# Four heads per interruption of TensorE in the attention, and a last weight chunk multiplied by row tile and column half ahead of each LayerNorm

## The reference, cut to what matters

```python
for i in range(DEPTH):                       # DEPTH = 2
    y = swa_sink_attention(...) if i % 2 == 0 else forgetting_attention(...)
    x = layer_norm(ALPHA * x + y, ln_g[i, 0], ln_b[i, 0])
    y = conv_ffn(x, w_up[i], conv_w[i], conv_b[i], w_down[i])
    x = layer_norm(ALPHA * x + y, ln_g[i, 1], ln_b[i, 1])
# in both mixers, per head and block of 128 queries:
#   p = exp(s - m);  p /= sum(p) (+ exp(sink - m));  o = p @ v
```

## Time and profile before

| | |
|---|---|
| median of three runs | 2142.12 us (2141.55 to 2143.27) |
| the profiled execution | 2144.39 us, of which the span from first to last instruction is 2142.6 us |
| PE busy | 2127.8 us, 99% of the span |
| DVE, ACT, POOL busy | 63%, 49%, 10% |
| granted clock of PE, mean | 0.999 of full speed |
| DMA, mean | 190 GB/s |

### The profile page before, as it was taken

The page is one execution under the profiler, slowest core; times in us unless marked ns, Lnnn a source line. Parts: engine busy times, 40 slices in busy tenths (PEclk is TensorE's granted clock), DMA queues, the critical chain, the costliest instruction groups (busy, mean ns, idle before and its releaser), DMA issues.

```text
span 2142.6 us, 40679 instructions
## 1 busy us (share of the span) xinstructions
PE 2127.8 (99%) x15160; PEld 1953.6 (91%) x15160; DVE 1341.0 (63%) x1829; ACT 1043.8 (49%) x1396; POOL 219.4 (10%) x211
## 2 busy tenths in 40 slices
PE   9999999999999999999999999999999999999998
PEld 8887899999999988888998997899999999988887
DVE  5676676766666654546576676576766666655554
ACT  4554465555555543335445444365555455544332
POOL 2000002220000000000251330002230000000000
PEclk9999999999999999999999999999999999999999
DMA  8554567666666656565665664657766666666563
GB/s 275 158 187 138 177 188 213 201 203 195 191 193 194 193 191 195 192 193 159 199 197 186 186 201 155 195 157 206 203 209 195 192 190 195 193 212 193 196 192 123
DMA packets 206603, 407.67 MB, mean 190 GB/s; under 512 B 12832, under 2 KB 13408, under 8 KB 206400
## 3 DMA queue, kind: packets, MB, share of 16 engines
q1 hardware_dynamic: 199680, 384.35, 58.6%
q0 software_dynamic: 5984, 20.74, 3.4%
q10 hardware_dynamic: 864, 1.57, 0.3%
HBM read 404.44 MB, written 2.18 MB: 190 GB/s over the span
## 4 chain that ended last, share of the span: by engine, by line
PE 96%; DVE 2%; ACT 1%; DMA 1%; issue 0%; DVEq 0%; ACTq 0%
PE ps L1302 19%; PE ps L1304 18%; PE ps L1305 18%; PE ps L1284 12%; PE ps L1286 12%; PE ps L1285 12%; PE ps L1477 1%; PE ps L1499 1%; PE ps L1486 1%; PE ps L1386 0%; PE ps L1410 0%; DMA raw<-in_a_w_o_dram 0%; DVE cg L882 0%; DVE w_lo L827 0%; PE ps L1508 0%
## 5 line engine op out<-in xcount | busy, mean ns | idle before, releaser
L827 DVE TENSOR_TENSOR w_lo<-raw,w_hi 128x1024 fp32r<-128x1024 f32 x725 | 914.7, 1267 | 618.3 <-ACT w_hi L534 616.6
L534 ACT ACTIVATE w_hi<-raw 128x1024 fp32r<-128x1024 f32 x725 | 768.6, 1060 | 929.5 <-PE ps L1305 489.1
L1302 PE MATMUL ps<-xh,w_lo 128*128 128x256 f32 x3572 | 993.6, 278 | 2.9 <-DVE xl L878 1.8
L1305 PE MATMUL ps<-xh,w_hi 128*128 128x256 f32 x3572 | 987.2, 276 | 0.0
L1304 PE MATMUL ps<-xl,w_hi 128*128 128x256 f32 x3572 | 987.2, 276 | 0.0
L1302 PEld LDWEIGHTS ps<-xh,w_lo 128*128 128x128 f32 x3572 | 670.6, 188 | 13.8 <-issue 8.1
L1305 PEld LDWEIGHTS ps<-xh,w_hi 128*128 128x128 f32 x3572 | 671.2, 188 | 0.0
L1304 PEld LDWEIGHTS ps<-xl,w_hi 128*128 128x128 f32 x3572 | 670.7, 188 | 0.0
L1286 PE MATMUL ps<-w_hi,hid_h 128*128 128x512 f32 x704 | 273.9, 389 | 0.0
L1285 PE MATMUL ps<-w_hi,hid_l 128*128 128x512 f32 x704 | 273.9, 389 | 0.0
L1284 PE MATMUL ps<-w_lo,hid_h 128*128 128x512 f32 x704 | 273.9, 389 | 0.0
(11 more groups left out here) (188 smaller groups left out, 1407.3 us busy)
## 6 DMA issues: line engine op xcount, KB each, us to landing
raw<-in_ffn_w_up_dram SPq DMA_DIRECT2D x352, 512.0 KB, 4.3
raw<-in_ffn_w_down_dram SPq DMA_DIRECT2D x176, 512.0 KB, 4.7
raw<-in_b_w_qkvf_dram SPq DMA_DIRECT2D x96, 512.0 KB, 4.3
raw<-in_a_w_qkv_dram SPq DMA_DIRECT2D x39, 512.0 KB, 4.3
raw<-in_a_w_o_dram SPq DMA_DIRECT2D x32, 512.0 KB, 4.4
raw<-in_b_w_o_dram SPq DMA_DIRECT2D x32, 512.0 KB, 4.7
bias<-rel_by_distance POOLq DMA_DIRECT2D x4, 1024.0 KB, 6.9
bias<-minus_cumulated_decay POOLq DMA_DIRECT2D x4, 1024.0 KB, 6.3
```

The source lines that it names most:

```text
L534: act.activation(w_hi[:, loc % RING], raw[:, loc % RING], ACT.Copy).then_inc(high_ready, 1)
L827: dve.tensor_tensor(w_lo[:, s], raw[:, s], w_hi[:, s].bitcast(FP32), ALU.subtract).then_inc(low_ready, 1)
L1302: pe.matmul(o, w_lo[:, slot, k % 2, cols], xh[:, k, :], start=(k == 0 and j % 2 == 0), stop=False, skip_group_check=True)
L1305: last = pe.matmul(o, w_hi[:, slot, k % 2, cols], xh[:, k, :], start=False, stop=(k == KT - 1), skip_group_check=True)
```

## The change

Three things.

1. **The attention is placed by fours.** PE's calls stand after slots 1, 5, 7, 11 and 13: scores of pairs 0 and 1; transposes of four heads; scores of pairs 2 and 3 and values of pairs 0 and 1; transposes of four heads; `turn_sums` and values of pairs 2 and 3. Scores and transposed probabilities of four heads now need four banks each. The sink's exponentials come after the fourth head's own instead of ahead of each head's, under a new semaphore. On DVE, `out_copy(1)`, `out_norm(1)` and `out_low(0)` move behind slot 14's split, and on ACT `spread_sums(1)` and `out_high(1)` move from slots 11 and 14 to 12 and 15. The output projection no longer waits for the whole third group before its first slot.
2. **The last two chunks ahead of a norm are multiplied by row tile and column half.** The last four k tiles are done for rows 0 to 127, then for rows 128 to 255 and the left 256 columns, then for the right 256 columns into another bank. DVE takes the statistics of the first row tile and of the left half meanwhile; after the last product it adds the right half, takes statistics of 256 columns and aggregates one row tile instead of two.
3. **The down projection's loop of two column groups is written out in PE's stream**, so that only the last group is ordered in this way.

```diff
+SCORES_AT = (1, 7)
+TURNED_AT = (5, 11)
+VALUES_AT = (7, 13)
...
+            def score_bank(j, idle):
+                return (S_BANK, S_BANK + 1, 2 * idle, 2 * idle + 1)[j % 4]
+            def turned_bank(j):
+                return (PT_BANK, S_BANK, S_BANK + 1, O_BANK)[j % 4]
...
+            def sink_exponentials(q, hc):
+                act.wait_ge(sinks_ready, 1)
+                for j in range(4):
+                    s = 4 * q + j
+                    ins = act.activation(esink[:, q, :, j], nmax[:, :, s], ACT.Exp, bias=sinks[:, 0, hc + s:hc + s + 1])
+                ins.then_inc(esinks_ready, 1)
...
             def attention_slot(k, hc, quads, kt, sink):            # ACT
+                for q in range(2):
+                    at = SCORES_AT[q]
+                    if k == at + 1:
+                        exponentials(4 * q, hc)
+                    if k == at + 2:
+                        exponentials(4 * q + 1, hc)
+                        exponentials(4 * q + 2, hc)
+                    if k == at + 3:
+                        exponentials(4 * q + 3, hc)
+                        if sink:
+                            sink_exponentials(q, hc)
...
             def attention_slot(k, hc, quads, kt, group, sink, idle):   # DVE
+                for q in range(2):
+                    at = SCORES_AT[q]
+                    if k == at:
+                        reduce_scores(4 * q, hc, group, sink, idle)
+                        reduce_scores(4 * q + 1, hc, group, sink, idle)
+                    if k == at + 1:
+                        reduce_scores(4 * q + 2, hc, group, sink, idle)
+                    if k == at + 2:
+                        reduce_scores(4 * q + 3, hc, group, sink, idle)
                 if k == 9:
                     one_over_sums(0, hc, sink)
+                    out_copy(0, hc, quads)
                 if k == 11:
                     one_over_sums(1, hc, sink)
+                for q in range(2):
+                    if k in (TURNED_AT[q], TURNED_AT[q] + 1):
+                        for c in range(2):
+                            copy_probs(4 * q + 2 * (k - TURNED_AT[q]) + c, hc)
...
             def residual(s, turn, used, n, pieces, tile0=0):       # DVE, rows 128 to 255
+                        if tile0 and half == 1:
+                            dve.wait_ge(chunks_used, used)
+                            dve.tensor_tensor(res[:, 1, part], res[:, 1, part], ps[:, RIGHT_BANK, 0:SEQ], ALU.add).then_inc(last_whole, 1)
+                            dve.wait_ge(last_whole, tile0)
+                        last = dve.bn_stats(stats[:, 1, bass.ds(n * 2 + half, 1), :].rearrange("p a b -> p (a b)"), res[:, 1, part])
...
             def group(s, turn, b4, loc0, lh, ll, nk=KT, before=None, tile0=None):   # PE
-                    if tile0 is last_tile0 and k >= nk - 2:
+                    if tile0 is last_tile0 and k >= nk - 4:
                         if k == nk - 1:
-                            for m in range(MT):
-                                for kk in (k - 1, k):
-                                    last = product(s, turn, kk, nk, lh, ll, loc % RING, tile0, (m,))
+                            for kk in range(nk - 4, nk):
+                                product(s, turn, kk, nk, lh, ll, (loc0 + kk // 2) % RING, tile0, (0,))
+                            for kk in range(nk - 4, nk):
+                                last = half_product(bank(s, 1)[:, 0:SEQ], 0, kk, False, kk == nk - 1, lh, ll, (loc0 + kk // 2) % RING)
+                            last.then_inc(last_left, 1)
+                            for kk in range(nk - 4, nk):
+                                last = half_product(ps[:, RIGHT_BANK, 0:SEQ], 1, kk, kk == nk - 4, kk == nk - 1, lh, ll, (loc0 + kk // 2) % RING)
+                                if kk % 2 == 1:
+                                    last.then_inc(chunks_used, 1)
...
             def scores(q, hc, quads, kv, first_waits, idle):       # PE, both pairs of a half
+                    pe.wait_ge(scores_used, hc + 4)
+                    pe.wait_ge(probsT_ready, hc + 4)
...
             def attention_slot(k, hc, quads, kv, first_waits, idle):   # PE
+                for q in range(2):
+                    if k == TURNED_AT[q]:
+                        for j in range(4):
+                            turn_probs(4 * q + j, hc, quads)
+                    if k == SCORES_AT[q]:
+                        scores(q, hc, quads, kv, first_waits, idle)
+                if k == VALUES_AT[0]:
+                    for i in (0, 1):
+                        times_values(i, hc, quads, kv)
+                if k == VALUES_AT[1]:
+                    pe.wait_ge(scores_used, hc + HG)
+                    pe.wait_ge(probsT_ready, hc + HG)
+                    turn_sums(0, quads)
+                    turn_sums(1, quads)
+                    for i in (2, 3):
+                        times_values(i, hc, quads, kv)
```

More of the change, by code:

```diff
@@ L595, in turned_copy, with exponentials @@
                    .then_inc(acc_free[s][0], 1)
-            def exponentials(s, hc, sink):
+            def exponentials(s, hc):
                 act.wait_ge(scores_used, hc + s + 1)
                 q, j = s // 4, s % 4
[L601 to L604, removed]
                 act.activation(prob[:, s % 4, 0:P], prob[:, s % 4, 0:P], ACT.Exp, scale=-1.0, bias=nmax[:, 0, s:s + 1],
@@ L1015, in residual @@
                     dve.wait_ge(acc_free[s][m], turn + 1)
-                    last = dve.bn_stats(stats[:, m, bass.ds(n, 1), :].rearrange("p a b -> p (a b)"), res[:, m, cols])
+                    if m == 0:
+                        last = dve.bn_stats(stats[:, 0, bass.ds(n, 1), :].rearrange("p a b -> p (a b)"), res[:, 0, cols])
+                        if tile0:
+                            own.link(last)
+                            last = dve.bn_aggr(mv[:, 0, :], stats[:, 0, 0:OUT_GROUPS, :].rearrange("p a b -> p (a b)"))
+                    for half in range(2 if m == 1 else 0):
+                        part = bass.ds(n * COLS + half * SEQ, SEQ)
+                        if tile0 and half == 1:
[3 more added lines that the diff above has]
+                        last = dve.bn_stats(stats[:, 1, bass.ds(n * 2 + half, 1), :].rearrange("p a b -> p (a b)"), res[:, 1, part])
+                        if half == 0:
+                            own.link(last)
                 return last
@@ L1035, in layer_norm @@
                 own.link(last)
[L1036 to L1038 removed]
+                own.link(dve.bn_aggr(mv[:, 1, :], stats[:, 1, :, :].rearrange("p a b -> p (a b)")))
                 dve.tensor_scalar(var[:, :], mv[:, :, 1], LN_EPS, None, ALU.add).then_inc(var_ready, 1)
@@ L1225, in mlp @@
                 for n in range(1, OUT_GROUPS):
-                    residual((n - 1) % 2, (t0, t1)[(n - 1) % 2] + (n - 1) // 2, CH_DOWN[l] + n * FC, n - 1, pieces)
+                    last = residual((n - 1) % 2, (t0, t1)[(n - 1) % 2] + (n - 1) // 2, CH_DOWN[l] + n * FC, n - 1, pieces)
+                    if l == DEPTH - 1:
+                        own.link(last)
                     if l < DEPTH - 1:
@@ L1276, in _, with product @@
         def _(pe):
-            def product(s, turn, k, nk, lh, ll, slot, tile0=None, tiles=range(MT)):
+            def product(s, turn, k, nk, lh, ll, slot, tile0=None, tiles=range(MT), right_ends=None):
                 for m in tiles:
@@ L1285, in product @@
                     pe.matmul(o, ll[:, k, rows], w_hi[:, slot, k % 2, :], start=False, stop=False)
-                    last = pe.matmul(o, lh[:, k, rows], w_hi[:, slot, k % 2, :], start=False, stop=(k == nk - 1))
+                    last = pe.matmul(o, lh[:, k, rows], w_hi[:, slot, k % 2, :], start=False, stop=(k == nk - 1 or m == 1 and k == right_ends))
                     if k == nk - 1 and m == 0 and tile0:
@@ L1289, in product, with half_product @@
                 return last
+            def half_product(o, half, k, start, stop, lh, ll, slot):
+                cols = slice(half * SEQ, (half + 1) * SEQ)
+                rows = slice(P, 2 * P)
+                pe.matmul(o, lh[:, k, rows], w_lo[:, slot, k % 2, cols], start=start, stop=False, skip_group_check=True)
+                pe.matmul(o, ll[:, k, rows], w_hi[:, slot, k % 2, cols], start=False, stop=False, skip_group_check=True)
+                return pe.matmul(o, lh[:, k, rows], w_hi[:, slot, k % 2, cols], start=False, stop=stop, skip_group_check=True)
             layer = [0]
@@ L1465, in turn_tok, with scores @@
                 last.then_inc(tok_turned, 1)
-            def scores(i, hc, quads, kv, first_waits):
-                if i == 0:
+            def scores(q, hc, quads, kv, first_waits, idle):
+                if q == 0:
                     first_waits()
```

105 lines of the change are left out of this document (42 added, 63 removed).

## The result

The changed kernel takes **2128.42 us** (median of four runs, 2127.3 to 2130.98). The kernel before, run beside it, takes 2142.69 (four runs, 2141.55 to 2143.54). The ratio is 0.9935, with a 95% interval of 0.9918 to 0.9953: 0.65% faster. The forecast was 2128.5. The profiled execution took 2127.92 us, of which the span is 2126.1.

A forecast was written before the change was run, and what follows sets the result against it. PE's stream bounds the kernel (busy 99%). Attention 10.6, layer 0's wait 1.1, `ol` 0.5 and norms 1.4 sum to 13.6 us, off a median of 2142.1: 2128.5 us, range 2126.5 to 2131 (2134.5 with the start-up and table-load rivals).

The forecast's parts named there:

- attention, runs instead of pairs, and layer 0's wait: Attention on PE: 1.32 us less per turn over eight turns, 10.6; layer 0's wait within transposes gone, 1.1.
- wait for `ol`: Ahead of the output projection's first slot: PE's single 0.5 us wait goes, as only groups finished earlier are asked for.
- norms: Ahead of the norms: 0.33 us gained on each of the first three, 0.45 at the last, together 1.4.
- a turn after: Attention on PE after the change: 10.0 us per turn, 9.03 and `turn_sums`, alike in both layers.
- The rival that pays start-up for each pair: Score and value pairs in the attention: each pays full start-up, 5.6 us less gain, 2134.1; chance 0.10.
- The slack: Attention: 0.9 us to spare before the fourth head's transposes, 1.3 between the last copy and slot 7's scores.
- Both rivals that needed a wait here: PE waits for four copies at 16 points: half a microsecond each, about 2136.5 (0.05); 0.85 each, 2142 (0.03).
- the rival of the split: DVE's split behind slot 4 or 10, held by ACT, delays the copies: 1.2 lost at each of 16, 2147.7; chance 0.05.
- Two of the three steps: Norms: half-width products take 2.71 us; variance at 1.6 after the dummies' start; table load holds the root until 1.95.
- 24 of 256 columns at 0.113 stand for twelve of 512: Ahead of the norms: splitting the products adds nothing on PE; the 24 take 2.71 us.
- The rival in which ACT stays closed for as long again: First three norms: a second 1.28 behind the table load puts the root at 3.2, 3.8 us in all, 2132.3; chance 0.03.

The follow-up runs named there:

- experiment 8: The changed kernel with the old wait for the whole third group put back ahead of the output projection's first slot; 2128.37 us (one execution).
- experiment 4: The changed kernel with its transposes two slots earlier, after slots 3 and 9; 2139.73 us (ten runs), ratio 0.9985 to before.
- experiment 2: The kernel before with parts 2 and 3 of the change and the attention's calls as they were; 2143.16 us (ten runs), ratio 1.0001.
- experiments 7, 9 and 10: The changed kernel with, in turn, half-width products reordered (2128.69 us), their rows from the first row tile (2128.65), both runs reading the left columns (2129.97).
- experiments 6 and 11: The changed kernel with ACT's table load ahead of its last split before the first three norms; 2129.63 us (one execution), then 2127.71 (five runs).

## Why the prediction was right

| term | forecast | measured |
|---|---|---|
| attention, runs instead of pairs, and layer 0's wait | 10.6 + 1.1 | 11.74 |
| wait for `ol` | 0.5 | 0.70 |
| norms | 1.4 | 1.0 |
| behind the last norm | nothing | 0.6 |
| sum | 13.6 | 14.0 |
| a turn after | 10.0 | 10.13 |

**The attention.** The step on which most of it hung was a row that the trace of before didn't have, a pair of scores directly behind a pair. It was taken at 0.65, its streaming. Measured: eight score matmuls cost 0.85 and sixteen 1.51, so the second pair 0.66; values 0.80 and 1.45, so 0.65. The rival that pays start-up for each pair is refuted. Twelve transposes with the product behind them in 1.23, the step from the last to the product 0.03, as forecast. A turn of layer 1 is 1.28 shorter (forecast 1.32), one of layer 0 by 0.32 more (forecast 0.27). Layer 0's turns now cost what layer 1's do: the wait inside the transposes has gone with its distance of four slots.

**The wait for `ol`.** It is gone, as forecast, but only 0.28 of its 0.70 through the relaxed condition, which the prediction gave as the reason (experiment 8); the other 0.4 came with `out_low` being earlier.

**Nothing waits for the four.** The slack was forecast at 0.9 for the fourth head's transposes and 1.3 for the copies. Measured: 99.1 less 97.26 is 1.8, and 102.25 less 100.59 is 1.7. Both rivals that needed a wait here are refuted; experiment 4 shows the price when the slack is used up (10.0 us). Of the rival of the split nothing came in the changed kernel; with the transposes a slot earlier a split was late twice, by 0.9 at most, beside POOL's work and not behind ACT's.

**The norms.** Two of the three steps held: the variance at 1.60 (forecast 1.6), the root held by the table load until 1.92 (1.95), a gain of 0.36 and at the last norm 0.49 (0.33 and 0.45). The mis-sized term is "24 of 256 columns at 0.113 stand for twelve of 512": they are 0.120 apart, which takes 0.6 us back. The net is 1.0 instead of 1.4. What the end of the program gained behind the last norm (0.6) had no term in the sum.

**The table load.** The rival in which ACT stays closed for as long again had 1.28 more behind each load. The rows show a load of 1.28 from 250.20 and the root at 251.50, 0.02 behind it. The drain that the Trainium skill ("ScalarE: Activation LUTs", What ACT_TABLE_LOAD costs) adds to a load would have put the root near 252.9 (an estimate with that section's 1.38); no load in these traces shows it: wherever an instruction was due behind one, it started 0.01 to 0.02 later.

**What was luck.** 14.0 lies this near to 13.6 because 0.4 too much at the norms nearly cancels 0.2 too little at `ol` and the 0.6 at the end that was not forecast. That the median fell within 0.1 of the forecast is luck too: it was 2128.42, and the same kernel in another five runs had 2129.1. The start of the program alone moves a run by up to 2 us.

## What to carry to other kernels

Switching TensorE between long streams and short foreign work cost here 0.23 us for each interruption and a start-up of 0.15 to 0.20 for each run of scores or values, and a second pair in the run paid neither: collect the short work as far as the other engines' results and the banks allow, and read from the timeline how much slack is left before the first of them is late. When a feeding engine is late, look at what ran beside it before you blame its queue: a split that takes 1.2 us alone took up to 2.9 beside POOL. An edit that splits a matmul in two should be charged by the measured rhythm of the new shape in its place, since a stream elsewhere with the same shape may run faster (0.113 against 0.120 here).

## What was not expected of the hardware

**DVE's splits slow down beside POOL.** In the kernel after, the split of 128 x 1024 takes 1.22 on average where POOL is idle during it (623 of 725), and 1.74 where POOL is busy for nine tenths of it or more (41), up to 2.92. The prediction charged 1.2 throughout; the distance of two chunks to PE nearly always covers the rest. The Trainium skill ("SBUF — State Buffer", Who interferes with whom) says that a DVE instruction with two SBUF inputs contends with a GpSimd instruction that reads SBUF; the split has two such inputs, and the traces agree with it as far as these durations go. No experiment here took POOL's work away.

**The rhythm of equal products differs by place.** Products of 256 columns come 0.113 apart in most stretches, 0.118 in some (in the turn shown, 47 distances from 92.58 to 98.11: 5.53 us), and 0.120 in the half-width ones, but for the first one or two distances of each norm (0.113 and 0.119). A stretch keeps its rhythm until the next interruption or wait, and the same stretch can have another one in another execution: the 192 products from 1101 on come 0.113 apart in the kernel before, and in experiment 2 at 0.113 up to a short wait and at 0.118 behind it. Over the whole program the slower distances cost 4.7 us in the kernel before, 4.5 in the kernel after and 7.3 in experiment 2 (turned and plain products together). For the half-width ones, most weight loads are reported as 192 ns long instead of 188. Their order, the rows and the columns are excluded by experiments 7, 9 and 10; the cause of either slower rhythm stays open.

**The first 5 to 11 us run slower, for a length that differs from one execution to the next.** PE's timeline of the kernel before, and then of the kernel after, near the start:

```profile
7.69 1.05 PE L1410 MATMUL ps<-w_hi,xl 128*128 128x512 f32 x2
8.54 1.05 PE L1410 MATMUL ps<-w_lo,xh 128*128 128x512 f32 x2
```

```profile
7.21 0.63 PE L1465 MATMUL ps<-w_hi,xl 128*128 128x512 f32 x2
7.67 0.63 PE L1465 MATMUL ps<-w_lo,xh 128*128 128x512 f32 x2
```

Two products of 512 columns take 0.85 in the first and 0.46 in the second. The view prints a granted clock of 1.00 for both stretches, but for the first that is no reading: the trace's record of the full clock begins at 10.34 us in the kernel before and at 5.14 in the kernel after, and there is none ahead of it. In the 14 traces it begins between 4.9 and 11.2 us. In the seven where it begins at 8.7 or later, neighbouring products are 0.43 apart ahead of it and 0.23 behind it; in the seven others it begins at 6.74 or sooner, and none are 0.43 apart. These distances stand to one another nearly as TensorE's two levels do, 1.2 and 2.4 GHz, so I read the slow stretch as the lower level, though no row says so. PE did the same in both kernels up to 4.5 us: dummies from 1.54 on.

It is not the change's: the kernel of experiments 6 and 11, the same program, came to the same product after 40.61 us in one execution and after 38.89 in the other, with the record beginning at 10.40 and 6.73. In the profiled executions of before and after these times are 40.38 and 38.76: 1.6 us of the spans' difference, and a reason why less than 2 us can't be told from a single time here.
